# Attention by pairs of heads on halves of the array, bias added by VectorE, and modulation sums drained in fours

## The reference, cut to what matters

```python
def modulation(cvec, lw):                      # six vectors per stream; 12 slabs of 512 columns per layer
    m = jax.nn.silu(cvec) @ lw["ada_w"] + lw["ada_b"]
...
def dense_context_attention(q, k, v):          # 128 context queries, 128 context keys
    s = jnp.einsum("bqhd,bshd->bhqs", qblk, k)
    p = jax.nn.softmax(s, axis=-1)
    return jnp.einsum("bhqs,bshd->bqhd", p, v)
...
def neighbourhood_attention(q, k, v, k_ctx, v_ctx, rpb):   # 256 latent queries, 256 latent + 128 cached keys
    s_loc = einsum(qb, kg) + bias              # learned relative bias, -inf outside the window
    s_ctx = einsum(qb, k_ctx)
    p = jax.nn.softmax(jnp.concatenate([s_loc, s_ctx], axis=-1), axis=-1)
    o = einsum(p_loc, vg) + einsum(p_ctx, v_ctx)
```

## Time and profile before

| what | value |
|---|---|
| median of three executions | 1465.18 us |
| the profiled execution, its own time | 1458.32 us |
| its span | 1456.5 us |
| TensorE matmul busy | 1305.1 us (90%) |
| VectorE busy | 552.7 us (38%) |
| ScalarE busy | 307.1 us (21%) |
| mean granted TensorE clock | 0.94 |

### The profile page before, as it was taken

One profiled execution on the slowest core, in us unless ns is written; L12 is line 12 of the kernel. 1 busy time (PEld: TensorE's weight loads), 2 busy tenths in 40 slices (PEclk: granted clock), 3 DMA queues, 4 the chain that ended last, 5 costly groups with the idle time before them and its releaser, 6 DMA issues.

```text
span 1456.5 us, 21322 instructions
## 1 busy us (share of the span) xinstructions
PE 1305.1 (90%) x8967; PEld 654.3 (45%) x8967; DVE 552.7 (38%) x1426; ACT 307.1 (21%) x747; POOL 91.7 (6%) x104
## 2 busy tenths in 40 slices
PE   4999997898997999898949999979999798989893
PEld 1565544674563333233316655447656333333331
DVE  1246974453253121212132579735525411111113
ACT  1237312122121101010002472122322110101000
POOL 0010011100001000000012000020000100000001
PEclk8899997999997999999978999979999899999997
DMA  9810145745843899999976003383493489999994
GB/s 341 238 58 0 58 151 139 245 172 207 313 144 138 304 393 394 390 391 374 374 256 189 1 3 107 101 217 124 157 346 132 166 306 391 397 391 389 367 364 161
DMA packets 172978, 341.90 MB, mean 235 GB/s; under 512 B 34495, under 2 KB 36935, under 8 KB 172871
## 3 DMA queue, kind: packets, MB, share of 16 engines
q1 hardware_dynamic: 165095, 313.86, 60.8%
q0 software_dynamic: 7776, 26.55, 5.2%
HBM read 318.63 MB, written 21.76 MB: 234 GB/s over the span
## 4 chain that ended last, share of the span: by engine, by line
PE 69%; DMA 13%; DVE 12%; issue 2%; SPq 1%; ACT 1%; POOL 0%; POOLq 0%; DVEq 0%; ACTq 0%
PE bank L491 65%; DMA arena<-in_moe_w_dram 8%; PE bank L494 4%; DVE arena L1587 3%; DVE ring L1587 3%; DMA ring<-in_ada_w_dram 2%; DVE small L1595 1%; DVE arena L1595 1%; DMA arena<-expert_dram,idx_row 1%; DMA raw_dram<-ring 1%; DMA arena<-tok_dram,idx 1%; DVE ring L1595 1%; ACT arena L1292 1%; DVE x L1595 1%; SPq L1163 1%
## 5 line engine op out<-in xcount | busy, mean ns | idle before, releaser
L491 PE MATMUL bank<-ring,arena 128*32 128x512 f32 (+1 forms) x3936 | 526.4, 595 | 28.7 <-DMA arena<-in_moe_w_dram 15.0
L1292 ACT ACTIVATE arena<-bank 128x512 f32<-128x512 f32 (+3 forms) x352 | 157.3, 480 | 835.2 <-PE bank L494 464.8
L491 PEld LDWEIGHTS bank<-ring,arena 128*32 128x32 f32 (+1 forms) x3936 | 162.3, 113 | 318.9 <-issue 318.7
L491 PE MATMUL bank<-ring,hT 128*128 128x512 f32 x576 | 254.4, 597 | 0.0
L491 PE MATMUL bank<-arena 128*32 128x512 f32 (+3 forms) x1088 | 241.8, 524 | 1.5 <-ACT arena L1292 1.5
L1587 DVE TENSOR_TENSOR arena<-arena,bank 128x512 f32<-128x512 f32 x32 | 21.8, 687 | 395.2 <-PE bank L491 395.2
L491 PEld LDWEIGHTS bank<-ring,hT 128*128 128x128 f32 x576 | 108.0, 192 | 126.0 <-issue 125.4
L491 PE MATMUL bank<-hT,ring 128*128 128x384 f32 x384 | 132.0, 500 | 0.1
L494 PE MATMUL bank<-const,arena 128*128 128x128 f32 x627 | 101.5, 290 | 28.1 <-ACT arena L1292 10.4
L494 PEld LDWEIGHTS bank<-const,arena 128*128 128x128 f32 x627 | 73.6, 146 | 109.4 <-issue 74.8
L491 PEld LDWEIGHTS bank<-arena 128*32 128x32 f32 (+2 forms) x1088 | 90.6, 139 | 40.5 <-issue 34.8
(11 more groups left out here) (124 smaller groups left out, 860.7 us busy)
## 6 DMA issues: line engine op xcount, KB each, us to landing
ring<-in_moe_w_dram SPq DMA_DIRECT2D x80, 2048.0 KB, 13.7
ring<-in_ada_w_dram SPq DMA_DIRECT2D x24, 2048.0 KB, 8.1
arena<-in_moe_w_dram SPq DMA_DIRECT2D x16, 2048.0 KB, 16.1
ring<-in_w_in_dram SPq DMA_DIRECT2D x14, 2048.0 KB, 9.7
expert_dram<-arena SPq DMA_DIRECT2D x24, 512.0 KB, 13.8
ring<-in_w_out_dram SPq DMA_DIRECT2D x4, 2048.0 KB, 7.9
arena<-in_na_rpb_dram SPq DMA_DIRECT2D x32, 96.0 KB, 4.7
tok_dram<-arena POOLq DMA_DIRECT2D x6, 512.0 KB, 4.0
```

The source lines that it names most:

```text
L491: return nc.tensor.matmul(out, lhsT, rhs, start=start, stop=stop)
L1292: return nc.scalar.activation(out, in_, func, **kw)
```

## The change

- **Steps of heads.** The 24 units become 10 steps: two of four context heads, and eight of two latent heads. `scores` issues the products of an even and an odd head in turn, so that they lie on rows 0 to 63 and 64 to 127 of the array and go to different banks. `weigh` gives the values as the stationary operand and the turned probabilities as the moving one, so that two heads write the two halves of bank 7's partitions, already in the order of `hT`.
- **Flipped queries.** `qk_cols` turns the latent queries with `flip` by products in place of transposes (the keys and context queries with `ident`, by products too). The bias is then a plain addition by VectorE on the score bank, ahead of the maximum.
- **Normalised turning.** VectorE takes the reciprocal of the row sums and writes `turn_a` (and `turn_b` for the context): `flip` or `ident` with its rows scaled. `probs_cols` is a product of the probabilities with it, so the transposes become full products. `outputs` and the `tr4` of its result go; ScalarE's `attended` copies bank 7 to `hT`.
- **Order.** A step has room for two rules and two points. Rule k runs at half-step k + 4. The points are 22 in place of 26. VectorE's `turns` of the next step stands behind the first rule and point of a step.
- **Sums by fours.** Four slabs accumulate in bank 3, each in its own two rows of a strip (the window in `silu_w` moves). VectorE copies, and TensorE turns, once for four slabs.

```diff
-UNITS_NA = TILES * HEADS
-POINTS = UNITS_NA + 2
+STEPS = [(0, 0, 4), (0, 4, 4)] + [(t, h, 2) for t in (1, 2) for h in range(0, HEADS, 2)]
+N_STEPS = len(STEPS)
+POINTS = 2 * N_STEPS + 2
 RULE_AT = 4
+SHARE = 4
 BLOCK = 32
 BLOCKS = P // BLOCK
...
-        rows_at[point + 1].append(s)
-        cols_at[point + 2].append(s)
+        if i % SHARE == SHARE - 1:
+            rows_at[point + 1].append(s)
+            cols_at[point + 2].append(s)
     return list(zip(products, rows_at, cols_at))
...
+def jobs_of(step):
+    _, h0, n = STEPS[step]
+    return [(2 * step + i, range(h0 + i, h0 + n, 2)) for i in range(2)]
+N_SCORES = 2 * N_STEPS
...
-                    pe.wait_ge(ada_taken, jobs["ada"])
+                at = jobs["ada"] % SHARE
+                if at == 0 and jobs["ada"]:
+                    pe.wait_ge(ada_taken, jobs["ada"] // SHARE)
                 w = wide(pre_slot[slab])
+                first = 2 * (SHARE - 1 - at)
                 for k in range(KC):
                     q = k % 4
-                    last = mm(bank[3][32 * q:32 * q + 32, :], silu_w[:, k, :], w[:, k, :], k < 4, k >= 4)
+                    last = mm(bank[3][32 * q:32 * q + 32, :], silu_w[:, k, first:first + 32], w[:, k, :],
+                              at == 0 and k < 4, at == SHARE - 1 and k >= 4)
                 last.then_inc(ada_full, 1)
                 jobs["ada"] += 1
                 slab_job[slab] = ("ada", jobs["ada"])
             def ada_cols(slab):
-                no = slab_job[slab][1]
+                no = slab_job[slab][1] // SHARE
                 pe.wait_ge(ada_taken, no)
                 b = dve_bank("mod_col", *slab)
                 for q in range(4):
-                    last = mm(b[:, 2 * q:2 * q + 2], mrow[:, (no - 1) % 2, q * P:(q + 1) * P], tab("pick"))
+                    last = mm(b[:, 8 * q:8 * q + 8], mrow[:, (no - 1) % 2, q * P:(q + 1) * P], tab("pick"))
                 last.then_inc(for_dve, 1)
             for i in range(EARLY):
                 ada_product(("ada", 0, i))
-                if i:
...
+                    for q in range(4):
+                        last = mm(b[:, q * P:(q + 1) * P], (z, z_k)[i][:, t, q * P:(q + 1) * P],
+                                  tab("flip") if i == 0 and t else ident)
+                    last.then_inc(for_act, 1)
                 transposed_norm(1, 0, 1)
                 arrived(pe, "win", l, 6)
...
+                def scores(step):
+                    t = STEPS[step][0]
                     keys = slice(0, P) if t == 0 else slice(P, 512)
...
+                    todo = [(act_bank("score", l, no), heads_) for no, heads_ in jobs_of(step)]
+                    for j in range(len(todo[0][1])):
+                        for b, heads_ in todo:
+                            h = heads_[j]
+                            half = slice(64 * (h % 2), 64 * (h % 2) + 64)
+                            out = b[:, j * P:(j + 1) * P] if t == 0 else b[:, 0:LAT + PAST]
+                            last = mm(out, qT[half, h // 2, t * P:(t + 1) * P], kT[half, h // 2, keys])
+                            if h == heads_[-1]:
+                                last.then_inc(for_act, 1)
+                def probs_cols(step):
+                    t = STEPS[step][0]
+                    pe.wait_ge(turn_ready, N_STEPS * l + step + 1)
+                    for i, (no, heads_) in enumerate(jobs_of(step)):
+                        b = act_bank("probs", l, no)
+                        for q in range(2 if t == 0 else 3):
+                            last = mm(b[:, q * P:(q + 1) * P], p_sb[:, (3 * i + q) * P:(3 * i + q + 1) * P],
+                                      (turn_a, turn_b)[q if t == 0 else 0][:, i])
+                        last.then_inc(for_act, 1)
+                def weigh(step):
+                    t, h0, n_heads = STEPS[step]
+                    pe.wait_ge(act_emptied, job["probs", l, jobs_of(step)[-1][0]])
+                    if h0 == 0 and (t or l):
                         pe.wait_ge(o_na_ready, 3 * l + t)
                     values = [v_sb[:, 0, :]] if t == 0 else [v_sb[:, 1, :], v_sb[:, 2, :], v_past]
...
+                    for i in range(0, n_heads, 2):
+                        for q, v in enumerate(values):
+                            for j in range(2):
+                                h = h0 + i + j
+                                at = (3 * j + (q if t else i // 2)) * P
+                                last = mm(bank[7][64 * j:64 * j + 64, (h // 2) * P:(h // 2 + 1) * P],
+                                          v[:, h * HD:(h + 1) * HD], pT[:, step % 2, at:at + P],
+                                          q == 0, q == len(values) - 1)
...
+                scores(0)
+                for step in range(N_STEPS):
+                    probs_cols(step)
+                    if step + 1 < N_STEPS:
+                        scores(step + 1)
+                    rule(2 * step - RULE_AT)
+                    point(2 * step)
+                    weigh(step)
+                    rule(2 * step + 1 - RULE_AT)
+                    point(2 * step + 1)
+                point(POINTS - 2)
+                point(POINTS - 1)
...
                     if j == 0:
                         pe.wait_ge(act_emptied, job["og", l, t])
+                        pe.wait_ge(o_na_ready, 3 * l + t + 1)
                     w = wide(pre_slot["wout", l, j])
...
+                def probs(step):
+                    t, h0, n_heads = STEPS[step]
+                    for i, (no, heads_) in enumerate(jobs_of(step)):
+                        b = filled("score", l, no)
+                        act.wait_ge(s_ready, N_SCORES * l + no + 1)
+                        for j, h in enumerate(heads_):
+                            at, keys = (j * P, CTX) if t == 0 else (0, LAT + PAST)
+                            last = f(p_sb[:, 3 * P * i + at:3 * P * i + at + keys], b[:, at:at + keys], ACT.Exp, bias=neg_max[:, t, h:h + 1], accum_out=row_sum[:, t, h:h + 1])
...
+                def probs_T(step):
+                    t = STEPS[step][0]
+                    if step >= 2:
+                        act.wait_ge(pv_done, N_STEPS * l + step - 1)
...
+                def attended(t):
+                    act.wait_ge(pv_done, N_STEPS * l + [s for s in range(N_STEPS) if STEPS[s][0] == t][-1] + 1)
+                    f(hT[:, 0:4, t * P:(t + 1) * P], bank[7][:].rearrange("p (k n) -> p k n", k=4)).then_inc(o_na_ready, 1)
...
+                for step in range(N_STEPS):
+                    probs_T(step)
+                    if step + 1 < N_STEPS:
+                        probs(step + 1)
+                    rule(2 * step - RULE_AT)
+                    if STEPS[step][1] == 0 and STEPS[step][0]:
+                        attended(STEPS[step][0] - 1)
+                    rule(2 * step + 1 - RULE_AT)
+                attended(TILES - 1)
...
+                vec.tensor_copy(mrow[:, (no // SHARE - 1) % 2, :], bank[3][:]).then_inc(ada_taken, 1)
             def ada_col(slab):
...
                 b = filled("mod_col", *slab)
-                tt(mods[:, layer, 4 * i:4 * i + 4, :], b[:, 0:8].rearrange("p (q s) -> p q s", s=2),
-                   over(cols[:, 0, 48 * layer + 4 * i:48 * layer + 4 * i + 4], 2), ALU.add).then_inc(dve_emptied, 1)
-                if i in (3, 9):
+                tt(mods[:, layer, 4 * i:4 * i + 4 * SHARE, :].rearrange("p (i q) s -> p i q s", q=4),
+                   b[:, 0:8 * SHARE].rearrange("p (q i s) -> p i q s", q=4, s=2),
+                   cols[:, 0, 48 * layer + 4 * i:48 * layer + 4 * i + 4 * SHARE].rearrange("p (i q) -> p i q", q=4)
+                   .unsqueeze(3).broadcast_to([P, SHARE, 4, 2]), ALU.add).then_inc(dve_emptied, 1)
+                if last in (3, 11):
                     dve.wait_ge(dve_emptied, job[("mod_col", *slab)])
...
+                def maxima(step):
+                    t, h0, n_heads = STEPS[step]
+                    for no, heads_ in jobs_of(step):
+                        dve.wait_ge(for_act, job["score", l, no])
+                        b = bank[4 + (job["score", l, no] - 1) % 3]
+                        if t == 0:
+                            vec.tensor_reduce(neg_max[:, 0, heads_.start:heads_.stop:2],
+                                              b[:, 0:2 * P].rearrange("p (h n) -> p h n", h=2),
+                                              AX, ALU.max, negate=True).then_inc(s_ready, 1)
+                        else:
+                            h = heads_[0]
+                            if h % 4 == 0:
+                                dve.wait_ge(bias_ready, 2 * l + h // 4 + 1)
+                            r0 = BIAS_ROWS - ROWS if t == 1 else 0
+                            link(tt(b[:, 0:LAT], b[:, 0:LAT], flat(bias[h // 4][:, h % 4, r0:r0 + ROWS, :]), ALU.add))
+                            vec.tensor_reduce(neg_max[:, t, h:h + 1], b[:, 0:LAT + PAST], AX, ALU.max,
+                                              negate=True).then_inc(s_ready, 1)
+                def turns(step):
```

(31 more changed lines are left out.)

110 lines of the change are left out of this document (17 added, 93 removed).

## The result

The changed kernel takes 1425.61 us, the median of four executions (1415.53 to 1427.51), against 1464.3 us of four executions of the kernel before. The ratio is 0.9724 with a 95% interval of 0.9672 to 0.9776: some 40 us faster. The forecast was 1430. The profiled execution took 1427.51 us, and the sum in the prediction had come to 1424.7 for it.

A forecast was written before the change was run, and what follows sets the result against it. TensorE was taken to set the pace, except in the hand-over-bound opening. Savings of 34.7 and 23.1 us less losses left 25.0 and 8.6, in all 33.6: 1424.7 profiled, 1431.6 by median, forecast 1430, range 1410 to 1450.

The forecast's parts named there:

- Sums and row waits: Modulation products: dropped column sums save 8.5 us in layer 0 and 5.7 in layer 1; layer 0's row-copy waits, 8.8, go.
- The steps by themselves: Attention steps: per layer 15.0 us saved on pairs and 2.4 on output transposes and wait, less 24.2 given back in all.
- A pair of heads: Latent steps on TensorE: 1.35 `probs_cols`, 0.9 `scores`, 0.7 `weigh`, so 2.95 us in place of 4.82.
- The bank addition: VectorE's bias addition on the score bank: 0.40 us; a rival with it at 0.69 or non-overlapping column halves had chance 0.22.
- The opening: Steps ahead of `rule(0)`: it comes 22.4 us after the first maximum, not 12.6; 7 us lost in layer 1, 4 in layer 0.
- `attended`: First `weigh` of tiles 1 and 2 waits for ScalarE to free bank 7: 3.5 us lost in layer 1, 0.7 in layer 0.
- Tail: From step 8, TensorE idles about 5 us behind VectorE's `rule(12)`: 4 us lost in layer 1, 5 in layer 0.
- By layer: Mixing stages, net gain after losses: 25.0 us in layer 0 and 8.6 in layer 1.
- the chain costs little: Rival for both mixing stages: only half of the 24.2 us given back is lost, 12 more gained, 1418; chance 0.17.
- The median: Whole kernel: the median stands 6.9 us above the profiled execution, so 1424.7 becomes 1431.6, given as 1430.
- The clock rival: Mixing stages: more TensorE idling lowers its granted clock to 0.75, costing 17 us a layer, nulling the gain; slower 0.04.

The follow-up runs named there:

- two experiments on the array's parts: Changed kernel with both score instructions on one half of the array, 1432.07 us (0.9772); changed kernel with `weigh` issued head by head, 1423.41 us (0.973).

## Why the prediction was right, point by point

- **Sums and row waits.** I gave them 14.2 + 8.8 = 23.0 us. The old order with fours and early row copies gains 25, of which the copies' place is 10 and the sums 15, each with some 5 to 10 us to either side. The terms agree with that. Its profile bears out layer 0, where the copies' place gives 6.2 us and the fours 9.3 (I had 8.8 and 8.5), but not layer 1, where the fours give 0.7 in place of 5.7 at a clock of 0.87 in place of 0.92. What the prediction did not see is that "only every fourth product can wait, and none of those stands behind that rule" is a property of the new order: in the old one a group of four ends there, and the fours alone gave 9.
- **The steps by themselves.** From the terms the steps come to 2 x (15.0 + 2.4) - 24.2 = 10.6 us. Each pair of rows in the first table with the same sums and the same place of the copies measures them, and the answers differ: 10 us with sums one by one and the copies ahead (9.5 in the profiles), 1 with the copies behind, 31 with fours behind, 21 with fours ahead and two more moves. The first and the last are free of the waits for rows. With some 10 us to either side both still hold the forecast, and they do not settle it closer. With sums one by one and the copies behind the rules the longer waits for rows, worth 20 us in that order against 10 in the old, eat the gain. The waits do not add to the other parts; their size depends on what VectorE has ahead of the copy.
- **A pair of heads** takes 3.32 us, not 2.95, which is 0.37 x 16 = 5.9 us too much gain. The mis-sized term is `probs_cols`, with 1.67 us in 10 of the 13 latent steps whose twelve instructions stand whole between their neighbours in the first profile (1.56 to 2.55 in the others), in place of 12 x 0.112 = 1.35. `scores` has 0.85 (I took 0.9), and `weigh` 0.80 (0.7). The prediction says that the gaps at a change of kind "are in both sums", but 1.35 is twelve bare intervals and holds none, so its remark that the sum would stay at 2.95 does not hold. In the trace the second of the twelve starts 0.21 us behind the first in place of 0.11, and the first score 0.34 behind the last (0.06 of it a wait). In the two experiments on the array's parts the mechanism held: the halves of rows overlap (0.6 us a step), and so do the halves of columns. The rule of the Trainium skill that tiles work independently, so that different tiles can load and multiply in parallel (TensorEngine Tiling (Array Packing), Key Properties), agrees with these two runs, with 1.07 and not 1.35 for `weigh` even without interleaving.
- **The bank addition** takes 0.43 us (I took 0.40).
- **The opening.** `rule(0)` came 21.97 and 22.48 us after the first maximum; I had 22.4. In layer 0 the third slab is multiplied at 264.85, after 262.97 before, so the opening costs 1.9 us there and not 4, and the slab's arrival covers the rest (1.34 of waiting for it are left, 1.56 before). From the third slab to the gate rows layer 0 takes 77.7 us, as forecast (77).
- **`attended`.** Waits of 2.41 + 1.38 in layer 1 and 0.56 in layer 0; I had 3.5 and 0.7. Taking them away changed the ratio by 0.0026, 4 us, with an interval of 7 us to either side.
- **Tail.** The wait is 4.99 us in layer 1, as forecast, and the slab product behind it ran at half clock (3.49 in place of 1.92). In layer 0 the slab arrived late by 2.88.
- **By layer.** Layer 0: 28.6 us, forecast 25.0. Layer 1: 6.4 and 8.3 in two profiles, forecast 8.6. The dearer pair takes 3.0 us from each layer. In layer 0 the opening and the late slab cost 1.9 + 2.9 = 4.8 in place of 4 + 5 = 9, so there the rival "the chain costs little" had a part. That the total came so near is luck in part, since these two wrong sizes have opposite signs.
- **The median.** I added 6.9 us to the sum, as the median of before stood above its profiled execution. The changed kernel's median stands 1.9 below its own. So the sum of 33.6 us of gain lies between the 30.8 of the profiled pair and the 38.7 of the medians, and neither settles it closer. The sum was 2.8 us under the profiled execution, and the 6.9 took the median 4.4 too high. The changed kernel's executions lie closer together (1415.5 to 1427.5 in eight) than those of before (1453.9 to 1476.8 in 49), as fewer executions would in any case. Whether the change narrows them was not tested.
- **The clock rival** did not come: the windows behind the openings were granted 0.94 and 0.93, where the kernel before had 0.92 and 0.97, although layer 1's opening has 0.75. TensorE was busy for 93 and 90% of them, more than the 80 to 87 that I expected. The clock was in play all the same: whole mixing stages were granted between 0.84 and 0.92 in the table, the least with the sums by fours alone and with sums one by one in the new order. These two have the low clock in layer 1 as well, where they wait for rows for 1 us or less, and the kernel before has 0.89 beside its 8.8 us of row waits. So the waits alone do not explain it, and no run tests what does.
- **Open.** The 4.2 us given back outside the mixing stages in the profiled pair. The time between layer 0's gate rows and layer 1's table load was 583.2 in both kernels and 576.9 in the second profile of the changed one, so it moves that much by itself.

## What to carry to other kernels

A producer that waits for a copy in another engine's queue pays for whatever stands ahead of the copy there. Put such a copy ahead of long work (here 10 to 20 us for one moved line), or make it rare. A long wait can be followed by slower products, as in the kernel with fours alone, so look at the clock behind it, too. Two changes that share a queue must be priced together: here each alone gave 1 and 9 us, both 40. Where a group of instructions of one kind stands between others, count the gaps on both sides (0.3 us for `probs_cols`), and not only the interval inside it. And an experiment that undoes one part shows what this part is worth beside the others, not what it gives alone; run both.

## What the runs showed of the hardware that I had not expected

TensorE stopped for 1.2 to 5.2 us in the midst of `rule(1)`'s 144 instructions of 32 x 32, with nothing in the profile to wait for. Timelines of TensorE, first of the changed kernel, then of its twin with sums one by one:

```profile
260.32 0.57 PE L505 MATMUL bank<-ring 32*32 32x32 f32 x43
262.12 1.39 PE L505 MATMUL bank<-ring 32*32 32x32 f32 x101 [1.23 <-issue]
```

```profile
263.22 1.54 PE L505 MATMUL bank<-ring 32*32 32x32 f32 x128 [0.91 <-issue]
269.96 0.43 PE L505 MATMUL bank<-ring 32*32 32x32 f32 x9 [5.20 <-issue]
```

The queues of DMA in this second kernel between 262 and 271 us:

```profile
q1 hardware_dynamic: 1136, 2.28, 72.2%
q8 instruction: 1, 0.02, 0.8%
q14 instruction: 1, 0.01, 0.2%
```

The tiny products are issued every 10 ns or so (96 in 1.0 us), and in the stretch of the gap one transfer of each instruction queue is under way beside the slabs. Such gaps are in the old kernel too (3.3 us in layer 1) and differ between executions, which is one reason why a single profile of this kernel does not settle 5 us.

The traces of all fourteen runs tell more. In their mixing stages 29 gaps of TensorE of 0.8 us or more have nothing to wait for. Each of the 29 ends 1.2 to 1.7 us after the end of a 16 KB transfer of q8, and only 8 to 10 such transfers fall into the 150 us around each stage. In the changed kernel one ends at 260.78 and TensorE goes on at 262.12, in its twin one ends at 268.47 and TensorE goes on at 269.96. That TensorE had run out of instructions and waited for these transfers fits all of them. No run changed the number or the place of the instructions to test it, and in the expert stages, where gaps of 1 to 3 us stand as well, the distance is not constant.
